# Front of a decoder step: the norm placed between two factor tables, injections ahead of responses, response transfers ahead of the last ten modulation blocks

## What is computed

```python
sh1, sc1, ga1, sh2, sc2, ga2 = split(silu(c) @ w_mod[layer] + b_mod[layer])  # and the kv and final rows: 16384 columns in all
h = rmsnorm(x, g_norm) * (1 + sc1) + sh1
lam_bar = exp(lam * dt);  b_bar = ((lam_bar - 1) / lam) * b
bu = einsum("blgp,gnp->blgn", h, b_bar)          # 64 groups of 16 channels, 64 states each
h_t = lam_bar * h_(t-1) + bu_t                   # along 512 rows
y = real(einsum("blgn,gpn->blgp", h_t, c)) + d_skip * h
out = a * sigmoid(g),  (a, g) = gelu(y) @ w_glu
```

## Time and profile before

| | us |
|---|---|
| median of 3 runs | 3589.09 |
| lowest and highest | 3577.5 and 3590.97 |
| span of the profiled execution | 3586.7 |
| first y round starts in that execution | 330.5 |
| loads of the last twelve modulation blocks begin | 244.3 |

### The profile page before, as it was taken

One profiled execution on the slowest core, in us unless ns is written; L12 is line 12 of the kernel. 1 busy time (PEld: TensorE's weight loads), 2 busy tenths in 40 slices (PEclk: granted clock), 3 DMA queues, 4 the chain that ended last, 5 costly groups with the idle time before them and its releaser, 6 DMA issues.

```text
span 3586.7 us, 62252 instructions
## 1 busy us (share of the span) xinstructions
PE 2614.0 (73%) x24910; PEld 955.6 (27%) x24910; DVE 2357.1 (66%) x5444; ACT 1226.6 (34%) x3819; POOL 1300.8 (36%) x1153
## 2 busy tenths in 40 slices
PE   4466898867766866657879997687686668666665
PEld 2355622403200400002224666141040013001000
DVE  8653387687776677556553444878867767765645
ACT  1222232434333333335432232343433343334333
POOL 5300033444444444434422431344444344443432
PEclk7667899967866866679999999686696678667667
DMA  8756699999999999999965045999999999999997
GB/s 329 222 127 220 273 390 411 396 420 407 412 420 420 395 421 420 405 420 410 410 232 154 30 175 228 418 397 413 418 403 421 420 420 407 419 420 402 417 421 320
DMA packets 215089, 1278.54 MB, mean 356 GB/s; under 512 B 54705, under 2 KB 60313, under 8 KB 67929
## 3 DMA queue, kind: packets, MB, share of 16 engines
q0 software_dynamic: 151552, 1109.46, 75.7%
q1 hardware_dynamic: 62688, 164.77, 13.1%
q10 hardware_dynamic: 576, 0.59, 0.1%
HBM read 1260.95 MB, written 11.43 MB: 355 GB/s over the span
## 4 chain that ended last, share of the span: by engine, by line
DMA 39%; PE 33%; DVE 18%; ACT 5%; issue 3%; SPq 1%; POOL 1%; DVEq 0%; ACTq 0%; PEldq 0%; POOLq 0%
DMA arena<-peer_uv,arena 36%; PE psum L2625 11%; DVE arena L2067 8%; PE psum L2570 6%; DVE arena L1654 3%; PE psum L2531 3%; PE psum L2990 2%; DVE arena L1663 1%; PE psum L2773 1%; DMA arena<-b_mod 1%; PE psum L2704 1%; ACT arena L1372 1%; ACT arena L1369 1%; DVE arena L1985 1%; DVE arena L2078 1%
## 5 line engine op out<-in xcount | busy, mean ns | idle before, releaser
L2625 PE MATMUL psum<-arena 32*32 32x512 f32 x16384 | 1534.0, 822 | 733.5 <-ACT arena L1372 729.6
L1130 POOL DMA_INDIRECT arena<-peer_uv,arena x1040 | 1130.0, 1087 | 1943.7 <-PE psum L2625 1555.7
L2067 DVE SCALAR_TENSOR_TENSOR arena<-arena 128x1024 f32<-128x1024 f32 x1040 | 1273.0, 1226 | 762.9 <-DMA arena<-peer_uv,arena 751.1
L1359 ACT ACTIVATE arena<-arena 128x1 f32<-128x1 f32 x1040 | 210.4, 202 | 1548.5 <-DVE arena L2067 1547.7
L2625 PEld LDWEIGHTS psum<-arena 32*32 32x32 f32 x16384 | 216.3, 119 | 1913.4 <-ACT arena L1372 1819.4
L1372 ACT ACTIVATE arena<-arena 128x32 f32<-128x32 f32 x1024 | 329.0, 321 | 33.4
L1369 ACT ACTIVATE arena<-arena 128x1 f32<-128x1 f32 x1040 | 306.0, 294 | 33.8
L2570 PE MATMUL psum<-arena 128*128 128x128 f32 x2048 | 264.5, 286 | 15.8 <-DMA arena<-peer_wq 14.7
L2570 PEld LDWEIGHTS psum<-arena 128*128 128x128 f32 x2048 | 246.4, 198 | 85.2 <-issue 83.6
L2428 PE MATMUL psum<-arena 128*9 128x128 f32 x2048 | 100.2, 376 | 110.1 <-DMA arena<-b_mod 110.1
L1654 DVE TENSOR_TENSOR arena<-arena 128x512 f32<-128x512 f32 (+9 forms) x206 | 156.3, 759 | 18.6 <-ACT arena L1198 5.7
(11 more groups left out here) (315 smaller groups left out, 2282.6 us busy)
## 6 DMA issues: line engine op xcount, KB each, us to landing
arena<-w_mod SPq DMA_DIRECT2D x64, 1024.0 KB
arena<-peer_wq SPq DMA_DIRECT2D x12, 2048.0 KB, 13.0
arena<-peer_uv,arena POOLq DMA_INDIRECT x1040, 10.4
arena<-w_glu SPq DMA_DIRECT2D x5, 2048.0 KB, 12.8
arena<-mod_rows SPq DMA_DIRECT2D x4, 1024.0 KB
arena<-w_o SPq DMA_DIRECT2D x1, 4096.0 KB
arena<-mod_rows SPq DMA_DIRECT2D x7, 512.0 KB, 4.8
arena<-x_after_layer SPq DMA_DIRECT2D x7, 512.0 KB
```

Of the source, the lines that this page charges most:

```text
L1130: pool.indirect_dma_start(ring[r], None, a[f"peer_uv{t // 5}"], bass.IndirectOffsetOnAxis(ap=ix, axis=0)).then_inc(landed[r], 16)
L1359: act.activation(col, col, ACT.Gelu_apprx_tanh).then_inc(s_gl, 1)
L2067: dve.scalar_tensor_tensor(out=u, in0=u, scalar=1.0, in1=h, op0=ALU.mult, op1=ALU.mult, accum_out=at(DOTS + (t % 2) * 2 * P + m, 1)).then_ ...
L2625: ins = pe.matmul(acc_of(t, i, c), diag[rows, r, :], ring[r][rows, D + 512 * c:D + 512 * (c + 1)], start=(m == 0), stop=last, skip_group_c ...
```

## The change

- SP loads only the first part of the S5 parameters for the tables, then the rest, then prompt rows, gain and sample rows, all ahead of block 0. The later loads of these go away. Two more small loads follow block 3.
- `bl` goes from POOL to DVE (seven slots of three operations; the eighth slot is two copies by ACT). The norm follows it, then `cl` (eight slots of three operations; the ninth is two copies by ACT). The 16 small `lamt` copies go from DVE to ACT. POOL keeps three clears and gets the load of `ssm_d`.
- `ROUNDS` becomes m0, m1, s, u0 to u3, i and m mixed, k0 to k3, y. The new round `s` transposes the sample rows on PE, in place of the way through DRAM.
- `MOD_FIRST = 10` blocks come first, and one block follows each of the twelve rounds in `MOD_AFTER`, in bank 7 alone. `MOD_ONE` is 22; ten blocks are left for the end.
- The i rounds are copied by ACT (16 linked copies each) and use three banks; i and s take the upper half, u, m and k the lower.
- `ksb` has a place for each of the four k rounds. SP issues the 32 response transfers after the clear of `toep` and ahead of the last ten blocks' loads; it no longer waits there for the i rounds or for the transfers to land. The y rounds and what reads the last state wait for them.

```diff
-MOD_ONE = 20
+MOD_FIRST = 10
+MOD_ONE = 22
...
-        ksb = [at(KSB + i * RG * P, RG * P, 0, GP).rearrange("p (g m) -> p g m", g=RG) for i in range(2)]
+        ksb = [at(KSB, RG * P, 32 * r, 32 * r + GP).rearrange("p (g m) -> p g m", g=RG) for r in range(G // RG)]
...
-        ROUNDS = ([("u", r) for r in range(NR)] + [("k", r) for r in range(NR)]
-                  + [("m", 0), ("m", 1), ("i", 0), ("m", 2), ("i", 1), ("m", 3), ("i", 2), ("i", 3)]
-                  + [("y", r) for r in range(NR)])
-        WHO = {"u": "A", "k": "A", "m": "A", "i": "V", "y": "V"}
+        ROUNDS = ([("m", 0), ("m", 1), ("s", 0)] + [("u", r) for r in range(NR)]
+                  + [("i", 0), ("m", 2), ("i", 1), ("m", 3), ("i", 2), ("i", 3)]
+                  + [("k", r) for r in range(NR)] + [("y", r) for r in range(NR)])
+        WHO = {"u": "A", "k": "A", "m": "A", "i": "A", "s": "A", "y": "V"}
+        MOD_AFTER = [("m", 0), ("m", 1), ("u", 0), ("u", 1), ("u", 2), ("u", 3), ("i", 0), ("i", 1), ("i", 2), ("i", 3),
+                     ("k", 0), ("k", 1)]
...
-            sp.dma_start(par, a["s5_par"]).then_inc(s_par, 16)
+            sp.dma_start(par, a["s5_par"][:, 0:NPAB]).then_inc(s_par, 16)
+            sp.dma_start(at(PARC, 2 * D), a["s5_par"][:, NPAB:NPAR]).then_inc(s_parc, 16)
+            x5v = a["x_prompt"].rearrange("(c s j) d -> s c (j d)", s=2, j=TC // 2)
+            for s in range(2):
+                sp.dma_start(at(CL, 4 * D, 64 * s, 64 * s + 64), x5v[s]).then_inc(s_x5, 16)
+            sp.dma_start(at(GBC, D), a["g_norm"][0:1, :].partition_broadcast(P)).then_inc(s_mods5, 16)
+            sp.dma_start(at(XS, D, 0, NB), a["x_sample"]).then_inc(s_x5, 16)
...
-            sp.wait_ge(s_tz, 1)
+            sp.dma_start(at(ST0, 2 * HALF * NB), a["state_g"]).then_inc(s_stg, 16)
+            sp.wait_ge(s_tz, 3)
+            sp.wait_ge(s_sk, 1)
             for r in range(NR):
                 wait_copied(sp, ("k", r))
                 for s in range(TC):
                     sp.dma_start(toep[GP * s:GP * (s + 1), RG * r:RG * (r + 1), GP * s:P],
-                                 ksb[r % 2][:, :, 0:P - GP * s]).then_inc(s_toep[r], 16)
-
-            wait_copied(sp, ("i", NR - 1))
-            for r in range(NR):
-                sp.wait_ge(s_toep[r], 16 * TC)
+                                 ksb[r][:, :, 0:P - GP * s]).then_inc(s_toep, 16)
             mod_loads(MOD_ONE, NMB, MOD_PLACES[1])
             for b in range(2):
                 sp.wait_ge(s_modmm[b], NMB)
+            sp.wait_ge(s_toep, 16 * TC * NR)
...
+            pool.wait_ge(s_h5, 2)
+            pool.memset(u2[:, :, CH:UC], 0.0).then_inc(s_tz, 1)
+            pool.dma_start(mod_a, a["ssm_d"].partition_broadcast(P)).then_inc(s_dld, 16)
+            wait_copied(pool, ("s", 0))
+            pool.memset(u2[96:P - GP, :, CH + NB:UC], 0.0).then_inc(s_tz, 1)
 
             for b in range(2):
                 pool.wait_ge(s_modmm[b], MOD_ONE)
             pool.memset(at(TOEP, G * P), 0.0).then_inc(s_tz, 1)
...
+                elif kind == "i":
+                    wide_i = ps[:, 0:2, 0:6 * UC].rearrange("p b (g c) -> p b g c", g=6)
+                    last_i = ps[:, 2, 0:4 * UC].rearrange("p (g c) -> p g c", g=4)
+                    for k in range(2):
+                        for gp in range(2):
...
+                            link(act.activation(sj[out, :, k, six].rearrange("p c (b g) -> p b g c", b=2),
+                                                src[:, :, :, 0:CH], ACT.Copy))
+                            link(act.activation(sj[out, :, k, two].rearrange("p c g -> p g c"), end[:, :, 0:CH],
+                                                ACT.Copy))
...
+                if key in MOD_AFTER:
+                    mod_copy(*mod_between(key), one=True)
...
+            wait_copied(dve, ("i", NR - 1))
+            dve.wait_ge(s_mm, round_no[("k", NR - 1)] + 1)
             link(dve.memset(hpx[:, 0, :], 0.0))
...
+            mod_products(0, MOD_FIRST, MOD_PLACES[0])
             for no, (kind, r) in enumerate(ROUNDS):
-                if no >= 2:
-                    wait_copied(pe, ROUNDS[no - 2])
...
+                if round_before(no):
+                    wait_copied(pe, round_before(no))
+                ps = half(key)
...
+                if kind == "s":
+                    pe.wait_ge(s_h5, 2)
+                    for g in range(G):
+                        pe.transpose(ps[0:GP, 0, NB * g:NB * (g + 1)], at(XS + GP * g, GP, 0, NB), ident[0:NB, 0:NB])
+                        ins = pe.matmul(ps[64:96, 0, NB * g:NB * (g + 1)], at(XS + GP * (g - 1), 2 * GP, 0, NB),
+                                        ident[0:NB, 0:NB], start=True, stop=True, skip_group_check=True)
...
+                if key in MOD_AFTER:
+                    mod_pair(MOD_PLACES[0], True)(*mod_between(key))
```

More of the change, by code:

```diff
@@ L158, in program @@
         pw_im = at(TAB + t9, t9).rearrange("p (t g) -> p t g", t=TC + 1)
[L159 to L163, removed]
+        ca = at(CAT, t9).rearrange("p (t g) -> p t g", t=TC + 1)
+        cb = at(CBT, TC * G).rearrange("p (t g) -> p t g", t=TC)
+        bb = at(TAB + 2 * t9, t9).rearrange("p (t g) -> p t g", t=TC + 1)
+        small = [at(TAB + 3 * t9 + i * G, G) for i in range(16)]
+        assert 3 * t9 + 16 * G <= 2 * RG * P and CAT + t9 <= ARENA
         bbar_re = at(TMP, D).rearrange("p (g q) -> p g q", g=G)
@@ L198, in program @@
         s_h5 = sem("s5_input_ready")
[L199 to L202, removed]
+        s_tz = sem("chunk_pad_and_response_cleared")
+        s_toep = sem("response_loaded")
         s_mm = sem("s5_round_products")
@@ L1219, in _ @@
[L1219 to L1228 removed]
+            act.wait_ge(s_x5, 48)
@@ new lines, in _, with mod_copy @@
+            for j in range(TC // 2):
+                link(act.activation(psum[:, 0:2, :].rearrange("p b n -> p (b n)"), x5[:, j, :], ACT.Square,
+                                    accum_out=stat[:, j:j + 1]))
+            act.activation(psum[0:NB, 0:2, :].rearrange("p b n -> p (b n)"), at(XS, D, 0, NB), ACT.Square,
+                           accum_out=stat[0:NB, 4:5]).then_inc(s_sq, 1)
+            def mod_copy(i, b, fresh=False, one=False):
+                if not fresh:
+                    act.wait_ge(s_modst[b], 16 * i)
+                act.wait_ge(s_modmm[b], 2 * i + 2)
+                for q in range(4):
+                    ins = act.activation(at(MODO + b * MB + MQ4 * q, MQ4, R32, R32 + NC9), mod_bank(b, q, one),
+                                         ACT.Copy)
+                    ins.then_inc(s_modev[b], 1)
+                act.wait_ge(s_modev[b], 4 * i + 4)
+                act.dma_start(mod_dram[:, bass.ds((2 * i + b) * MB, MB)],
+                              at(MODO + b * MB, MB, R32, R32 + NC9)).then_inc(s_modst[b], 16)
@@ new lines, in mod_evac @@
+            def mod_evac(first, last):
+                pairs(act, first, last, mod_copy)
+            mod_evac(0, MOD_S5)
+            act.wait_ge(s_bb, 1)
+            act.activation(bl[0:64, :, TC - 1, :], bbar_re[0:64], ACT.Copy).then_inc(s_blp, 1)
+            act.activation(bl[64:P, :, TC - 1, :], bbar_im[64:P], ACT.Copy).then_inc(s_blp, 1)
+            act.wait_ge(s_tabs, 1)
+            for gp in range(2):
+                rows = slice(64 * gp, 64 * gp + 64)
+                for m, t in enumerate((TC, 1)):
+                    for k, (src, sign) in enumerate(((pw_re, 1.0), (pw_re, 1.0), (pw_im, -1.0), (pw_im, 1.0))):
+                        c0 = (4 * m + k) * HALF
+                        act.activation(lamt[rows, c0:c0 + HALF], src[rows, t, gp:G:2], ACT.Copy, scale=sign
+                                       ).then_inc(s_lam, 1)
@@ L1865, in _ @@
             tx = sj_tmp
+            dve.wait_ge(s_stg, 16)
             for k, fac in ((0, nli), (1, li)):
@@ L2418, in _, with mod_pair @@
         def _(pe):
-            def mod_products(first, last, places):
+            def mod_pair(places, one=False):
                 def pair(i, b, fresh=False):
```

292 lines of the change are left out of this document (132 added, 160 removed).

## The result

The changed kernel takes 3566.3 us (median of 6 runs, 3564.2 to 3573.1), the kernel before 3589.5 (6 runs beside them): a ratio of 0.9949, with a 95% interval of 0.9929 to 0.9969. A second set of 10 runs gave 3569.4 against 3585.7 for the kernel before on the same chip (13 runs), a ratio of 0.9959 (0.9946 to 0.9971). So the change gives 0.4 to 0.5%, 16 to 23 us by the medians. Forecast were 3569 and -20.

A forecast was written before the change was run, and what follows sets the result against it. The front up to y was taken to wait for weights over DMA. Block 21 at 203, plus 34 for transfers, 65 for ten blocks and 9.4 for copies, gave y at 311 against 330.5: -20 us, 3569, range 3542 to 3592.

The forecast's parts named there:

- Up to block 9: Start of the front: x and gain loaded ahead of block 0 shift block 9 by 10 us, from 80.8 to 91.
- Tables and norm: DVE work before the rounds: bl by 71, norm by 87, cl by 118 us, all in time for their rounds.
- Rival 5: First rounds: m0 waits for bl or s for the norm; chance 0.05 together with rival 4.
- s: Sample-row round on PE: 192 instructions at 0.065 us make 12; 11 us taken, between 6 and 20.
- u0 to u3: Four u rounds, each with a block: held at the load floor of 6.0 us each, 24 us.
- i0 to i3: Injection rounds waiting for ACT's copies: three steps of 13 us and a last of 9, 48 us.
- Rival 3: ScalarE's injection copies: 0.4 us more each cancels the gain, 0.8 makes it 18 us slower, 3607 us; chance 0.05.
- The response transfers: Between block 21 and the last stream: clear 6.9, issues 25, waiting weights 2, so 34 us paid in full.
- The end of the front: Last stream to y: ten blocks take 65 us, the states' copies 9.4, so y starts at 311.
- Rival 1: Front: PE stays slow and transfers are dear, so no change, 3588 us, or 3596 with both; chance 0.20.
- Rival 2: Front: PE fast, issues shortest, y at 283, -47 us, 3542; chance 0.20 including what lies between it and the forecast.
- Rival 4: Behind y: DMA-bound gathers give back what y gains, 3589 us; chance 0.05 together with rival 5.

The follow-up runs named there:

- x_late: Changed kernel with x, gain and sample rows loaded behind block 3 instead of ahead of block 0: y at 308.7 us, ratio 0.9938 to the kernel before.
- s_order: Changed kernel with the s round's 64 transposes first, then its 64 products, instead of in turn: y at 302.3 us, ratio 0.9917 to the kernel before.
- toep_pool: Changed kernel with the 32 response transfers issued by GpSimd behind its clear instead of by SyncE: y at 304.2 us, ratio 0.9946 to the kernel before.
- no_inter: Changed kernel with blocks 10 to 21 all before the first round, none between rounds: y at 373.7 us, ratio 1.0092 to the kernel before.
- with all four: Changed kernel with GpSimd-issued response transfers, later x, injection copies split over two engines and s round in two groups: 3525.6 us, ratio 0.9811 to the kernel before.
- s_half: Changed kernel with 56 of the s round's 64 products left out, so values differ: y at 301.0 us, ratio 0.9916 to the kernel before.

## Why the prediction was right

The time (3569 forecast, 3566 and 3569 measured), the sign and the mechanism held: block 21 was done at 203.96, forecast 203, and y started at 313.4 and 309.5, forecast 311. But several terms were off and cancelled, so that the sum met block 21 within 1 us is luck: block 9 was 4 us late and the s round 8 too long, against 2, 2, 3 and 3.5 too much for m, u, i and k.

- **Up to block 9**: +14.2 us in the first profile and +13.2 in the second, forecast +10. The term was 9.2 + 1.9 - 1. Block 0 started 12.4 us later, for 11.1, and x_late confirms that all 12 were x and its companions. The 1 us that the sample state was to give back behind block 3 didn't come: TensorE's wait between blocks 3 and 4 was 14.9 and 14.0 us, before 13.4 and 13.5. Two more rows are loaded in it, which the prediction took at nothing; how much of the growth is theirs wasn't tested.
- **Tables and norm**: bl was written by 62 and the norm done by 77.5, cl by 107. m0 came at 94.9 without a wait. Forecast: 71, 87 and 118 at the latest. Rival 5 is out.
- **m0, m1**: 11.1 us, forecast 13; the blocks ran at 1.94.
- **s**: 19.1 (18.6 in the second profile), forecast 11. This term was the worst. The row of eight equal small transposes gave 0.065 for each of 192 instructions, 12; s_order, the same instructions in two groups, needs 8.6, so that price was on the safe side where they don't take turns. A row of equal instructions doesn't show what changing kinds costs. The measured time lies at the dear end of the range given, 6 to 20.
- **u0 to u3**: 21.6, forecast 24, the load floor; TensorE had two blocks waiting after the s round.
- **i0 to i3**: steps of 11.0, 10.8 and 12.2, forecast 13; all four 44.7, forecast 48. The copies were right (7.1 us a round, forecast 7.5; 0.82 + 0.38 + 0.20 + 0.18 for a quarter). The first two rounds were 3.80 at the upper clock and not 5.7, the others 5.39 and 7.12. The last, "only its round and block", took 10.7 to k0, forecast 9, with the round at 7.12. Rival 3 would have needed 0.4 us more for each copy; they were not dearer than forecast, and it is out.
- **k0, k1**: 12.5, forecast 16, again the clock.
- In sum 109 us for the twelve steps, forecast 112, from a start 4 us later.
- **The response transfers**: 6.9 for the clear, then 28.1 from the first issue to the first weights, forecast 25 and 2 for weights that wait behind them. The sum held, 35 for 34, but not its parts: the issues were 3 dearer, and the ten blocks behind them took no longer than forecast. That they are "paid in full" because of the queue is not the whole cause either: in toep_pool, off the queue, they still cost most of it, through the 17 us of engine time.
- **The end of the front**: ten blocks in 64.7 (forecast 65) and 9.5 behind them (9.4).
- **Rival 1** (slow clock) didn't come, but no_inter shows that its rounds are real: without blocks between them the i rounds take 7.1 us each. The loss of 0.9% there is in the main that of the loads no longer under the rounds, not of the clock. **Rival 2** (everything fast) is what the edits approach: with all four, y comes at 275, below the 283 of that rival. **Rival 4** is out: what y gained was found at the end, 17 of 24 us in the first profile; whether a few us more came behind y is open.

## What to carry to other kernels

Between two streams of weights, look for what can be done under the loads, and put blocks between rounds that wait for copies: it fills TensorE's waits. The overlap was most of the 62 us that this was worth here, and rounds at the upper clock some 16 of it (an estimate). In such a chain of rounds price every step at both clocks, and look at the copies that free the accumulators: splitting them over two engines gave nearly as much as the whole change. And don't price a row of small instructions from a row of equal ones where they take turns.

## What the runs showed of the hardware

- Small fp32 products and transposes that take turns cost 0.06 to 0.08 us for each change: 64 + 64 take 18.6 to 19.1 us in turn and 8.6 in two groups.
- The four i rounds took 7.1 us each without blocks between them (granted clock 0.57), 3.80, 3.80, 5.39 and 7.12 with blocks (0.86 in their stretch), and 3.7 to 3.8 each with the copies split as well (1.00). In s_half, with blocks, three of four took 7.0 to 7.1.
- ScalarE and VectorE reading different partitions of the same accumulators at once: 0.80 to 0.87 us for 64 x 384 on either, for ScalarE no slower than in the kernel after, where it copies alone (0.80 to 0.94).
- Transfers inside SBUF of 16 partitions with runs of 64 to 512 bytes moved 140 GB/s of full engine time (2.4 MB, 0.49 of 35 us); GpSimd issued them at 0.55 us each, SyncE at 0.87, and 1.0 with two blocks' loads ahead (mean of 32).
